# Slot lists of a mixture-of-experts router: ranks written 128 columns wide and in two parts, half the products, and the last transposes ahead of the last tile's first logits

## The chip, the cores and the metric

The kernel runs on one core of a Trainium2 chip. The metric is the device time of one execution in microseconds, as a median of several runs. The engines are TensorE (PE, with its weight loads shown apart as PEld), VectorE (DVE), ScalarE (ACT), GpSimd (POOL) and SyncE (SP), which here only issues transfers. TensorE's clock has two levels, 2.4 and 1.2 GHz; the profile shows what was granted as 1.00 and 0.50.

## The reference

Two layers of a bidirectional encoder over 512 tokens of width 1024, float32 throughout. Each layer mixes the tokens (four head groups and an output projection) and then runs a mixture of experts: a group of 8 experts is chosen of 4, and in it the two best experts of 8. What matters here is the routing:

```
pg = softmax(ht @ rg_w + rg_b);  pg_top, g_sel = top_k(pg, 1)
le = (ht @ re_w + re_b).reshape(T, 4, 8);  le_sel = le[chosen group]
top_v, top_i = top_k(le_sel, 2)
expert_idx = g_sel * 8 + top_i;  gate = pg_top * softmax(top_v)
# tokens are grouped by expert; for each expert:
y = (silu(xe @ w_gate[e]) * (xe @ w_up[e])) @ w_down[e]
x = x + g2 * (sum of the two experts' y, times their gates)
```

The kernel keeps 64 places (`CAP`) for the tokens of each of the 32 experts in its main pass. What overflows is handled behind it.

## The kernel before, in words

All engines run their own program; an order written out by hand and semaphores tie them together. Both layers have the same stages: modulation sums and projections, the Hyena filters, attention, the output projection `w_out`, the router, and then the stage of the 32 experts.

**End of the output projection (L842 to L866).** For each of four tiles of 128 tokens TensorE makes two halves of `w_out`; VectorE adds them to the residual `x_tok` (L2097, L2098) and raises `x_half` and then `x_ready`. TensorE turns the finished rows of a tile with `transpose_rows` (L640, four transposes for each half of the row), ScalarE copies them into `hT` (L1370), and eight products with `r_w` (`logits`, 36 columns) give a tile's logits. For the last tile TensorE's program was: `logits(b, 3, 0)`, then the transposes of the second half of the row, which wait for `x_ready`, then `logits(b, 3, 1)`, which waits until ScalarE has copied them. ScalarE computes the square sum of the same rows (L1523) ahead of that last copy. VectorE writes the normalised rows of the last tile (L1838) and then takes its logits (L2084).

**Choice and ranks (L2131 to L2162).** On VectorE a chain of some 20 small instructions finds the two experts of every token and writes them as one-hot rows `m1`, `m2`; their sum `msum` goes to TensorE (L870 to L874, bank `before`), which counts how many tokens with the same expert stand before each. From this VectorE makes each token's rank in its expert (`rank_tmp`, `rank_f`, L2158 and L2159), and compares the rank with 0 to 63 (L2160): `rank_is` holds for each of the 2 choices and 4 tiles a 128x64 matrix with a one at the token's rank. It lay in `pr_r` at 2304.

**The slot lists (L876 to L891).** A product of `rank_is` (stationary) with `id_of` (32 columns, one for each expert) puts the token's number at its place. It is made twice, once into rows 0 to 63 and once into rows 64 to 127 of the bank `slots`, as both halves of a row of 1024 values are gathered as rows of their own: `h_rows` are half rows. Eight pairs of such products add up. VectorE turns the result into `slot_i` (L2164), and POOL starts the gathers of the experts' tokens (L1689). Behind `slots`, VectorE makes the gates and `w_of` (L2167 to L2173), and TensorE makes the same products with `w_of` into `wslots`, followed by four products of `ones` with `msum` (the counts).

**The stage of the experts (L894 on).** It begins when VectorE has emptied `wslots` (L2179, L2180) and the first gather has landed: transposes (L900), a copy by ScalarE (L1534), 16 products with `w_gate` and 16 with `w_up` in 32 pieces of 256 columns, and so on. SP loads the weights, 3 MB for each expert, into four or six slots of `big`, `x_tok` and `mod`; a load waits until TensorE has used the slot's last content (L1152, L1158, L1164).

A float32 product shows as two MATMUL and two LDWEIGHTS instructions in the trace; a transpose as one of each.

Of the kernel before, what the change touches and what calls it, by code (L numbers as in the profile page):

```python
# [20 lines left out]
ALU = mybir.AluOpType  # L21
# [3 lines left out]
P = 128  # L25
DEPTH, D, S = 2, 1024, 512
NT = S // P
# [16 lines left out]
NE, NG, EPG, F = 32, 4, 8, 256  # L44
TURN = [EPG * (i % NG) + i // NG for i in range(NE)]
CAP = 64
# [39 lines left out]
def trunk(nc, a, out):  # L86
# [9 lines left out]
    with ctx:  # L96
# [15 lines left out]
        pr_r = sb("pr_r", [P, 3072])  # L112
# [12 lines left out]
        def at(buf, off, *dims, rows=P):  # L125
            n = int(np.prod(dims))
            v = buf[0:rows, off:off + n]
            if len(dims) == 1:
                return v
            names = "abcd"[:len(dims)]  # L130
            return v.rearrange(f"p ({' '.join(names)}) -> p {' '.join(names)}", **{names[i]: dims[i] for i in range(len(dims))})
# [63 lines left out]
        xg, yg = at(ht_r, 0, 4, S), at(ht_r, 2048, 4, S)  # L195
        xT = at(pr_r, 0, 2, KT * CAP)
        sil, act_h, act_T = at(pr_r, 1024, 2, F), at(pr_r, 1536, 2, F), at(pr_r, 2048, 2, P)
        rank_is = at(pr_r, 2304, 2, NT, CAP)
        rank_tmp = at(pr_r, 1792, 2, NT, NE)
        shift_w, shift_sum = at(pr_r, 2560, KT, 36), at(pr_r, 2560 + KT * 36, 36)  # L200
        next_parts = [part[0:4, :], at(pr_r, 2304, ADA, rows=4), at(mix_r, 0, ADA, rows=4)]
# [2 lines left out]
        def rb(*dims, rows=P):  # L204
# [8 lines left out]
        id_of, chosen, w_of = (row_tab[:, :, :, j] for j in range(3))  # L213
# [9 lines left out]
        rank_f = rb(2, NT)  # L223
# [35 lines left out]
        iota_c, iota_e = misc[:, 0:CAP], misc[:, 0:NE]  # L259
# [24 lines left out]
        dft_in, mod_in, ln2_in, mla_w_in, fill_in, rw_in, hot_ready, ov_i = (  # L284
            sem(n) for n in "dft_in mod_in ln2_in mla_w_in fill_in rw_in hot_ready ov_i".split())
# [231 lines left out]
        def _(pe):  # L517
            def mm(o, l, r, start=True, stop=True):
                return nc.tensor.matmul(o, l, r, start=start, stop=stop)  # L519
# [4 lines left out]
            def layer(l):  # L524
# [23 lines left out]
                if l == 0:  # L548
# [31 lines left out]
                    b = A.bank("fp")  # L580
# [9 lines left out]
                    b = V.bank("fn")  # L590
                    for j in range(4):
                        last = mm(b[:, j:j + 1], f_tmp[:, j * P:(j + 1) * P], ones[:, 0:1])
# [4 lines left out]
                    b = V.bank("fnb")  # L597
                    for j in range(4):
                        last = mm(b[:, j * P:(j + 1) * P], f_tmp[:, j * P:(j + 1) * P], ident[:, :])
# [25 lines left out]
                def transpose_rows(n, halves=range(2)):  # L625

                    t = n % NT
                    if n < NT:
                        pe.wait_ge(hrow_ready, 2 * NT * l + n + 1)
                    src = h_tok[:, t % 2, :] if n < NT else x_tok[:, t, :]  # L630
                    for half in halves:
                        if n >= NT:
                            pe.wait_ge(x_ready if half else x_half, NT * l + t + 1)
                        b = A.bank(f"hT{n}{half}")
                        for j in range(4):
                            if n < NT:
                                rows = src.rearrange("p (c k) -> p k c", k=KT)[:, 4 * half + j]
                            else:
                                rows = src.rearrange("p (h c j) -> p h j c", h=2, j=4)[:, half, j]
                            last = nc.tensor.transpose(b[:, j * P:(j + 1) * P], rows, ident[:, :])  # L640
                        last.then_inc(ready_a, 1)
# [15 lines left out]
                for m in range(6):  # L657
                    b = V.bank(f"d{m}")
# [173 lines left out]
                def logits(b, t, half):  # L832

                    taken(pe, f"hT{NT + t}{half}")
                    for k in range(4 * half, 4 * half + 4):
                        last = mm(b[:, 0:36], hT[:, k, t * P:(t + 1) * P], r_w[:, k, :], k == 0, k == KT - 1)
                    if half:
                        last.then_inc(ready_v, 1)
# [22 lines left out]
                            logits(b, t - 1, 1)  # L861

                b = V.bank(f"lg{NT - 1}")
                logits(b, NT - 1, 0)
                transpose_rows(2 * NT - 1, (1,))
                logits(b, NT - 1, 1)  # L866

                pe.wait_ge(m_ready, l + 1)
# [4 lines left out]
                    last = mm(b[:, n * NE:P], ones[:, :], ms[:, 0:P - n * NE], False, n == NT - 1)  # L873
                last.then_inc(ready_v, 1)  # L874

                pe.wait_ge(hot_ready, l + 1)  # L876
                b = V.bank("slots")
                for k in range(2):
                    for t in range(NT):
                        for rows in (slice(0, CAP), slice(CAP, P)):  # L880
                            last = mm(b[rows, 0:NE], rank_is[:, k, t], id_of[:, k, t], k + t == 0, k + t == NT)
                last.then_inc(ready_v, 1)
                pe.wait_ge(wtab_ready, l + 1)
                b = V.bank("wslots")
                for k in range(2):
                    for t in range(NT):
                        for rows in (slice(0, CAP), slice(CAP, P)):
                            mm(b[rows, 0:NE], rank_is[:, k, t], w_of[:, k, t], k + t == 0, k + t == NT)
                for t in range(NT):
                    last = mm(b[:, NE:2 * NE], ones[:, :], msum[:, t], t == 0, t == NT - 1)  # L890
                last.then_inc(ready_v, 1)  # L891
# [877 lines left out]
        def _(v):  # L1769
# [22 lines left out]
            def layer(l):  # L1792
# [356 lines left out]
                for o, mk in ((o1, m1), (o2, m2)):  # L2149
# [7 lines left out]
                cum_p = b[:, 0:P].rearrange("p (t e) -> p t e", t=NT)  # L2157
                step(TT(rank_tmp, chosen, twice(cum_p), ALU.mult))  # L2158
                step(RED(rank_f.rearrange("p k t -> p (k t)"), both(rank_tmp), X, ALU.add))  # L2159
                TT(both(rank_is), iota_c.unsqueeze(1).to_broadcast([P, 2 * NT, CAP]),  # L2160
                   rank_f.rearrange("p k t -> p (k t)").unsqueeze(2).to_broadcast([P, 2 * NT, CAP]), ALU.is_equal).then_inc(hot_ready, 1)
                took(STT(out=cum, in0=cum_p, scalar=float(NE), in1=iota_e.unsqueeze(1).to_broadcast([P, NT, NE]), op0=ALU.mult, op1=ALU.add))  # L2162
                b = V.take("slots")
                took(TS(slot_i[:, :], b[:, 0:NE], empty_half, None, ALU.add))  # L2164
# [162 lines left out]
```

## Time and profile before

| | |
|---|---|
| median of 3 runs | 1444.33 us (1442.68 to 1446.61) |
| the profiled execution | 1447.86 us, its span 1446.0 us |
| granted clock, mean | 0.964 |
| PE busy | 1295.3 us (90%) |
| PEld busy | 754.9 us (52%) |
| DVE busy | 642.6 us (44%) |
| ACT busy | 356.9 us (25%) |
| POOL busy | 274.5 us (19%) |
| DMA | 338.85 MB, mean 234 GB/s |

Times in the rows are microseconds from the start of the span. Busy time of PE says that something was in the array, not that it ran at its peak. 1.9 us lie outside the span.

### The profile page before, as it was taken

The numbers are of one execution on the slowest core, as the hardware profiler recorded it, in microseconds if no ns is written. First come the engines' busy times: TensorE is split into PE (matmuls) and PEld (weight loads), VectorE is DVE, ScalarE is ACT, GpSimd is POOL, SyncE is SP. The second block draws the span as 40 slices with busy tenths as digits, with TensorE's granted clock in tenths as the row PEclk, the third lists the DMA queues.
The fourth block names the chain that finished last, engine by engine and source line by source line (L and its number), as shares of the span: only waits on it lengthen the run. The fifth ranks groups of instructions, "written<-read, shape, count | busy, mean of one in ns | idle before, by whom it ended". The sixth has DMA issues, their size and how long they took to land.

```text
span 1446.0 us, 17998 instructions
## 1 busy us (share of the span) xinstructions
PE 1295.3 (90%) x6672; PEld 754.9 (52%) x6672; DVE 642.6 (44%) x1353; ACT 356.9 (25%) x839; POOL 274.5 (19%) x291
## 2 busy tenths in 40 slices
PE   5899999999997897898999999999999789997872
PEld 1445655766645554444444565566664555554441
DVE  4644547687535221433144263769853522221112
ACT  1411121556501111111221211145650111111111
POOL 0200310000100442332230022000010044332232
PEclk8999999999998899999999999999999789999997
DMA  8801222446675889999971132344137589999984
GB/s 289 323 36 58 87 106 103 181 161 208 223 294 204 326 311 370 409 407 404 380 280 46 59 145 76 118 174 146 59 117 288 204 314 388 399 401 402 400 328 145
DMA packets 100836, 338.85 MB, mean 234 GB/s; under 512 B 30084, under 2 KB 34820, under 8 KB 75498
## 3 DMA queue, kind: packets, MB, share of 16 engines
q1 hardware_dynamic: 75208, 307.55, 54.7%
q0 software_dynamic: 15072, 16.85, 5.2%
q10 hardware_dynamic: 10468, 13.28, 2.6%
q8 instruction: 55, 0.90, 0.2%
q14 instruction: 33, 0.27, 0.1%
HBM read 326.16 MB, written 29.00 MB: 246 GB/s over the span
## 4 chain that ended last, share of the span: by engine, by line
PE 80%; DVE 9%; ACT 4%; issue 4%; DMA 2%; POOL 1%; SPq 0%; ACTq 0%; POOLq 0%; DVEq 0%
PE bank L519 73%; PE bank L914 2%; PE bank L803 2%; DVE pr_r L2201 2%; ACT pr_r L1543 2%; DVE pr_r L2204 1%; PE bank L640 1%; DMA big<-in_ada_w_dram 1%; DVE small L2050 1%; DVE big L1783 1%; DMA x_tok<-x_rows 0%; POOL small L1623 0%; ACT ht_r L1469 0%; DVE ht_r L2045 0%; DVE part L1992 0%
## 5 line engine op out<-in xcount | busy, mean ns | idle before, releaser
L519 PE MATMUL bank<-big,pr_r 128*64 128x256 f32 (+2 forms) x3032 | 424.3, 399 | 44.7 <-DVE pr_r L2204 22.6
L519 PEld LDWEIGHTS bank<-big,pr_r 128*64 128x64 f32 (+1 forms) x3032 | 253.6, 152 | 184.9 <-issue 96.4
L519 PE MATMUL bank<-big,ht_r 128*128 128x512 f32 (+3 forms) x832 | 315.3, 555 | 3.0 <-ACT ht_r L1496 2.2
L519 PEld LDWEIGHTS bank<-big,ht_r 128*128 128x128 f32 (+1 forms) x832 | 147.0, 189 | 134.7 <-issue 119.4
L519 PE MATMUL bank<-big 128*128 128x256 f32 (+4 forms) x496 | 163.0, 466 | 8.7 <-ACT big L1343 3.6
L1698 POOL DMA_INDIRECT x_rows<-ht_r,slot_i x64 | 102.1, 1596 | 323.0 <-DVE ht_r L2207 309.5
L2201 DVE TENSOR_TENSOR pr_r<-pr_r,bank 64x256 f32<-64x256 f32 x65 | 27.5, 423 | 220.7 <-ACT pr_r L1543 215.7
L1543 ACT ACTIVATE pr_r<-bank 64x256 f32<-64x256 f32 x64 | 24.2, 378 | 405.4 <-PE bank L519 405.4
L519 PEld LDWEIGHTS bank<-big 128*128 128x128 f32 (+2 forms) x496 | 89.5, 192 | 48.3 <-issue 25.4
L2207 DVE SCALAR_TENSOR_TENSOR ht_r<-bank,mix_r,mod 128x512 f32<-128x512 f32 x65 | 48.8, 751 | 132.6 <-PE bank L519 132.6
L519 PE MATMUL bank<-ht_r,big 128*128 128x512 f32 x192 | 85.0, 605 | 1.4 <-ACT ht_r L1370 1.4
L1473 ACT ACTIVATE ht_r<-bank,small 128x512 f32<-128x512 f32 x96 | 65.4, 685 | 62.1 <-DVE small L2050 58.2
L1689 POOL DMA_INDIRECT ht_r<-h_rows,slot_i x64 | 68.1, 1064 | 47.8 <-DVE slot_i L2164 28.9
L2050 DVE TENSOR_REDUCE small<-bank 128x1 f32<-128x512 f32 x96 | 63.2, 686 | 18.1 <-PE bank L519 17.0
L803 PEld LDWEIGHTS bank<-ident,ht_r 128*128 128x128 f32 x336 | 39.0, 140 | 52.1 <-DVE ht_r L2061 19.7
L519 PEld LDWEIGHTS bank<-ht_r,big 128*128 128x128 f32 x192 | 37.1, 194 | 48.3 <-issue 46.3
L1661 POOL COPY ht_r<-small 128x1 f32<-128x1 f32 x32 | 5.5, 185 | 296.3 <-PE bank L803 296.3
L803 PE MATMUL bank<-ident,ht_r 128*128 128x128 f32 x336 | 54.9, 280 | 4.1 <-ACT ht_r L1473 1.3
L1992 DVE SCALAR_TENSOR_TENSOR part<-big,small,part 128x768 f32<-128x768 f32 x56 | 57.0, 1019 | 2.1 <-DVE mix_r L2075 0.2
L1534 ACT ACTIVATE pr_r<-bank 128x512 f32<-128x512 f32 x65 | 38.8, 597 | 49.0 <-PE bank L900 49.0
L1481 ACT ACTIVATE pr_r<-bank 128x512 f32<-128x512 f32 (+2 forms) x96 | 50.6, 534 | 0.0
L900 PE MATMUL bank<-ident,ht_r 128*128 128x128 f32 x260 | 49.1, 312 | 0.9 <-DVE mix_r L2180 0.9
(308 smaller groups left out, 1262.1 us busy)
## 6 DMA issues: line engine op xcount, KB each, us to landing
big<-in_moe_w_gate_dram SPq DMA_DIRECT2D x59, 1024.0 KB, 17.5
big<-in_moe_w_up_dram SPq DMA_DIRECT2D x59, 1024.0 KB, 21.4
big<-in_moe_w_down_dram SPq DMA_DIRECT2D x59, 1024.0 KB, 25.3
big<-in_ada_w_dram SPq DMA_DIRECT2D x16, 3072.0 KB, 12.0
big<-in_w_in_dram SPq DMA_DIRECT2D x4, 3072.0 KB, 14.1
big<-in_w_out_dram SPq DMA_DIRECT2D x4, 2048.0 KB, 8.6
mod<-in_ada_b_dram SPq DMA_DIRECT2D x12, 512.0 KB, 9.4
x_tok<-in_moe_w_gate_dram SPq DMA_DIRECT2D x6, 1024.0 KB, 16.0
```

The source lines that it names most:

```text
L519: return nc.tensor.matmul(o, l, r, start=start, stop=stop)
L803: last = nc.tensor.transpose(b[:, j * P:(j + 1) * P], prob[:, ms[0] % PB, j * P:(j + 1) * P], ident[:, :])
L900: last = nc.tensor.transpose(bank[b][:, j * P:(j + 1) * P], rows, ident[:, :])
L1473: A_(prob[:, n % PB, :], b[:, :], ACT.Exp, bias=nm[:, n:n + 1], accum_out=rs[:, n:n + 1]).then_inc(taken_a, 1)
L1481: A_(probT[:, n % TB, 0:w], b[:, 0:w], ACT.Copy).then_inc(taken_a, 1)
L1543: A_(sil[0:CAP, b, :], bank[2 + b][0:CAP, 0:F], ACT.Silu).then_inc(silu_ready, 1)
L1689: g.indirect_dma_start(out=xg[:, e % 4, :], out_offset=None, in_=half_rows(h2_rows), in_offset=bass.IndirectOffsetOnAxis(ap=slot_i[:, TURN ...
L1698: g.indirect_dma_start(out=half_rows(x_rows), out_offset=bass.IndirectOffsetOnAxis(ap=slot_i[:, TURN[e]:TURN[e] + 1], axis=0), in_=yg[:, e ...
L1992: return STT(out=part[:, :], in0=w, scalar=c_full[:, k:k + 1], in1=part[:, :], op0=ALU.mult, op1=ALU.add)
L2050: nc.vector.tensor_reduce(nm[:, n:n + 1], bank[4 + of(f"S{n}")[1] % 4][:, :], X, ALU.max, negate=True).then_inc(nm_ready, 1)
L2201: return TT(act_h[0:CAP, b, :], sil[0:CAP, b, :], bank[2 + b][CAP:P, 0:F], ALU.mult)
L2207: return STT(out=yg[:, b, :], in0=bank[6 + b % 2][:, :], scalar=w, in1=g2, op0=ALU.mult, op1=ALU.mult)
```

## The change

`rank_is` becomes 128 columns wide for each choice and tile, the ranks' comparison standing in it twice side by side, and moves to `pr_r` at 0. It is written by two instructions, one for each choice, of 128x512 elements each, and `hot_ready` is raised after each. One product now fills all 128 rows of the bank where two had filled 64 each: 8 in place of 16 in `slots`, and 8 in place of 16 in `wslots`. In the order of TensorE the transposes of the last tile's second half row come in front of `logits(b, 3, 0)`.

```diff
-        rank_is = at(pr_r, 2304, 2, NT, CAP)
+        rank_is = at(pr_r, 0, 2, NT, P)
...
                 b = V.bank(f"lg{NT - 1}")
+                transpose_rows(2 * NT - 1, (1,))
                 logits(b, NT - 1, 0)
-                transpose_rows(2 * NT - 1, (1,))
                 logits(b, NT - 1, 1)
...
-                pe.wait_ge(hot_ready, l + 1)
                 b = V.bank("slots")
                 for k in range(2):
+                    pe.wait_ge(hot_ready, 2 * l + k + 1)
                     for t in range(NT):
-                        for rows in (slice(0, CAP), slice(CAP, P)):
-                            last = mm(b[rows, 0:NE], rank_is[:, k, t], id_of[:, k, t], k + t == 0, k + t == NT)
+                        last = mm(b[:, 0:NE], rank_is[:, k, t], id_of[:, k, t], k + t == 0, k + t == NT)
                 last.then_inc(ready_v, 1)
                 pe.wait_ge(wtab_ready, l + 1)
                 b = V.bank("wslots")
                 for k in range(2):
                     for t in range(NT):
-                        for rows in (slice(0, CAP), slice(CAP, P)):
-                            mm(b[rows, 0:NE], rank_is[:, k, t], w_of[:, k, t], k + t == 0, k + t == NT)
+                        mm(b[:, 0:NE], rank_is[:, k, t], w_of[:, k, t], k + t == 0, k + t == NT)
...
-                TT(both(rank_is), iota_c.unsqueeze(1).to_broadcast([P, 2 * NT, CAP]),
-                   rank_f.rearrange("p k t -> p (k t)").unsqueeze(2).to_broadcast([P, 2 * NT, CAP]), ALU.is_equal).then_inc(hot_ready, 1)
+                for k in range(2):
+                    TT(rank_is[:, k].rearrange("p t (h c) -> p t h c", h=2), iota_c.unsqueeze(1).unsqueeze(2).to_broadcast([P, NT, 2, CAP]),
+                       rank_f[:, k].unsqueeze(2).unsqueeze(3).to_broadcast([P, NT, 2, CAP]), ALU.is_equal).then_inc(hot_ready, 1)
```

## Rows read from the trace of the kernel before

**Rows 1.** Page, part 4: the chain that ended last, by engine, by line.
```profile
PE 80%; DVE 9%; ACT 4%; issue 4%; DMA 2%; POOL 1%; SPq 0%; ACTq 0%; POOLq 0%; DVEq 0%
```

**Rows 2.** Timeline, layer 0's last logits; start, length, engine, line, what, idle before.
```profile
451.57 2.76 PE L519 MATMUL bank<-mix_r,ht_r 128*128 128x36 f32 x24
...
452.50 0.69 DVE L2098 TENSOR_TENSOR x_tok<-x_tok,pr_r 128x512 f32<-128x512 f32 x1
...
454.17 0.70 PE L640 MATMUL bank<-ident,x_tok 128*128 128x128 f32 x4
454.19 0.19 ACT L1523 ACTIVATION_READ_ACCUMULATOR big<-x_tok 128x1 f32 x1
...
454.91 0.60 ACT L1370 ACTIVATE ht_r<-bank 128x512 f32<-128x512 f32 x1 [0.54 <-PE bank L640]
455.38 1.41 DVE L1838 SCALAR_TENSOR_TENSOR big<-pr_r,small,mod 128x512 f32<-128x512 f32 x2 [0.65 <-POOL small L1623]
455.56 1.92 PE L519 MATMUL bank<-mix_r,ht_r 128*128 128x36 f32 x8 [0.69 <-ACT ht_r L1370]
...
457.52 0.26 DVE L2084 SCALAR_TENSOR_TENSOR mix_r<-bank,small,mix_r 128x36 f32<-128x36 f32 x1 [0.72 <-PE bank L519]
```

**Rows 3.** Timeline of PE, cut short: five of those eight products.
```profile
455.56 1.28 PE L519 MATMUL bank<-mix_r,ht_r 128*128 128x36 f32 x5 [0.69 <-ACT ht_r L1370]
```

**Rows 4.** Timeline, layer 0, from the ranks to the token list.
```profile
465.33 0.42 DVE L2159 TENSOR_REDUCE mix_r<-pr_r 128x8 f32<-128x256 f32 x1
465.79 0.69 DVE L2160 TENSOR_TENSOR pr_r<-misc,mix_r 128x512 f32<-128x512 f32 x1
466.40 0.28 DVE L2162 SCALAR_TENSOR_TENSOR mix_r<-bank,misc 128x128 f32<-128x128 f32 x1
466.53 1.92 PE L519 MATMUL bank<-pr_r 128*64 128x32 f32 x32 [1.69 <-DVE pr_r L2160]
468.57 0.25 DVE L2164 TENSOR_SCALAR slot_i<-bank,small 128x32 int32<-128x32 f32 x1 [1.90 <-PE bank L519]
```

**Rows 5.** Timeline, layer 0, from the first gather to the first expert.
```profile
469.76 1.32 POOL L1689 DMA_INDIRECT ht_r<-h_rows,slot_i  x1 [14.48 <-DVE slot_i L2164]
...
470.57 1.92 PE L519 MATMUL bank<-pr_r 128*64 128x32 f32 x32 [2.11 <-DVE pr_r L2173]
...
472.42 1.92 PE L519 MATMUL bank<-mix_r,ones 128*128 128x32 f32 x8
...
473.96 0.33 SPq L1158 DMA_DIRECT2D x_tok<-in_moe_w_up_dram  x1
...
474.81 1.10 PE L900 MATMUL bank<-ident,ht_r 128*128 128x128 f32 x4 [0.47 <-DVE mix_r L2180]
...
476.60 5.07 PE L519 MATMUL bank<-big,pr_r 128*64 128x256 f32 x32 [0.69 <-ACT pr_r L1534]
```

**Rows 6.** Windows: stretch, its length, busy time (count) of PE, PEld, DVE, ACT, POOL, granted clock, DMA share, GB/s.
```profile
466.50:468.50 2.00, 1.92 (x32) 1.79 (x32) 0.18 (x1) 0.00 (x0) 0.00 (x0) 0.50 1.02 430
...
472.40:474.40 2.00, 1.93 (x10) 1.78 (x8) 0.03 (x1) 0.00 (x0) 1.41 (x2) 0.50 0.36 107
...
1168.00:1169.00 1.00, 1.00 (x8) 0.57 (x6) 0.00 (x0) 0.00 (x0) 0.00 (x0) 0.52 0.36 148
1169.00:1170.00 1.00, 1.00 (x10) 0.56 (x7) 0.04 (x1) 0.30 (x1) 0.00 (x0) 1.00 0.00 0
...
1172.00:1173.00 1.00, 1.00 (x8) 0.41 (x6) 0.00 (x0) 0.00 (x0) 0.00 (x0) 1.00 1.08 459
```

**Rows 7.** Timeline, layer 1: last logits, first expert, first load of the next expert.
```profile
1142.08 1.92 PE L519 MATMUL bank<-mix_r,ht_r 128*128 128x36 f32 x8 [0.69 <-ACT ht_r L1370]
...
1163.11 6.54 PE L519 MATMUL bank<-big,pr_r 128*64 128x256 f32 x32 [0.69 <-ACT pr_r L1534]
...
1169.69 0.33 SPq L1152 DMA_DIRECT2D big<-in_moe_w_gate_dram  x1
```

**Rows 8.** SP's transfers in layer 0's expert stage, timeline.
```profile
535.59 0.33 SPq L1164 DMA_DIRECT2D big<-in_moe_w_down_dram  x1
...
545.71 0.36 SPq L1152 DMA_DIRECT2D big<-in_moe_w_gate_dram  x1
```

**Rows 9.** The chain that ended last, layer 0: a wait for weights.
```profile
564.18 4.83 issue
```

**Rows 10.** The same chain in layer 1: waits for weights, and 32 products at full clock.
```profile
1379.27 2.46 issue
1381.73 3.69 PE bank L519 x32
```

**Rows 11.** Windows of layer 1's expert stage, columns as in rows 6.
```profile
1170.00:1255.00 85.00, 77.25 (x547) 43.26 (x548) 17.70 (x37) 11.41 (x24) 38.41 (x31) 1.00 1.02 388
...
1305.00:1395.00 90.00, 70.02 (x472) 41.12 (x468) 15.31 (x33) 10.25 (x22) 28.16 (x22) 0.98 1.02 402
```

## The prediction

> **What bounds the kernel now.** I began with the page's chain of the work that ended last: TensorE carries 80% of it, VectorE 9% [rows 1]. That average says little about the router, so I read its stretch in the timeline, once for each layer. There the chain goes from engine to engine with nothing beside it: TensorE waits for VectorE's ranks, VectorE waits for the token list, TensorE waits for the gates, and the experts wait for both [rows 2, 4, 5]. Whatever is added between the last logits and the first expert is added to the time, unless the stage of the experts takes it back. The reader should look at the square brackets at the end of the rows: they name who was late. Then I read the granted clock of the stretch in the windows view: it is 0.50 (1.2 GHz) while both lists are made [rows 6].
>
> The sum is made against the profiled execution, 1447.86 us with a span of 1446.0 us, 3.5 us (0.24%) above the median of 1444.33 us. A difference of a few us is carried over to the median as it is.
>
> **The products for the lists.** A product is two instructions in the trace. Before, the token list takes 32 of them with 64 columns of weights each, in 1.92 us [rows 4]: 0.06 us each. After, it takes 16 with 128 columns of weights. What such an instruction costs here is shown three times. The counts behind the weight list have the very shape of the new products, 128 columns of weights and 32 moving ones: 8 in 1.92 us at clock 0.50 [rows 5, 6]. The last tile's logits, each with weights of its own: 8 in 1.92 us, and the first five of them in 1.28 us [rows 2, 3]. So one starts every (1.92 - 1.28) / 3 = 0.213 us, four times the cost of a narrow one, whose 32 start within 1.92 us. PEld is busy for 1.79 us with the 32 narrow loads and for 1.78 us with the 8 wide ones [rows 6]: the weight loads fill the time in both, and halving the count of the products does not halve it. The new list takes 1.92 + 8 x 0.213 = 3.62 us. Against 1.92 us that is **+1.70 us** a layer.
>
> The weight list is followed by the counts without a gap, 470.57 to 474.34 = 3.77 us in all [rows 5]. After it is 24 wide instructions in a row, 1.92 + 16 x 0.213 = 5.33 us: **+1.56 us** a layer. The difference from 1.70 is the step from narrow to wide, which disappears.
>
> The Trainium skill has rules on both sides. "TensorEngine Tiling (Array Packing)", section "Key Properties", says that tiles of the array work independently and can load weights and multiply in parallel, which speaks against merging the two halves; the trace agrees, with 32 narrow instructions in the time of 8 wide ones. Its section "Instruction Overhead" puts about 60 cycles on every matmul, which by itself would favour fewer of them; the wide rows, four times the narrow ones, do not follow it.
>
> **Ranks in two parts.** Each of the two new instructions writes 128x512 elements, as the old one did in 0.69 us [rows 4]. So the first is done when the old one was, and TensorE starts no earlier. The second ends some 0.6 us later and is needed when four products are through, 8 x 0.213 = 1.70 us after the start: hidden by them. Behind it on VectorE is only `cum` (L2162, 0.28 us), and then the wait for the token list, which now has 3.62 us of cover. Cost 0; if the broadcast over four dimensions made both instructions slower, the first of them would count, and I allow 0.0 to 0.3 us. If nothing covered it, the second would cost 0.6 us.
>
> **Transposes first.** Before, TensorE works on logits from 451.57, eight of whose 24 instructions belong to the last tile, and starts the transposes at 454.17; the rows are ready at 452.50 + 0.69 = 453.19 [rows 2]. The 16 instructions of the tile before end at about 453.3, so the transposes can start there and end at 454.0. But ScalarE is busy with the square sum until 454.19 + 0.19 = 454.38, and copies at 454.91 now: the copy comes at about 454.39, **0.52 us** earlier, not 0.87. The first logits of the last tile (8 x 0.11 us) fit in until 454.9, in front of the copy's end at 455.0. The second half is then 0.52 us earlier, and VectorE with it, as it is free from 455.38 + 1.41 = 456.79 and waits until 457.52 [rows 2]. At most 0.7 us can be gained, as VectorE's own rows come next. In this execution the clock fell just as these logits ran (they took 1.92 us in both layers [rows 2, 7]); where it falls later they take about half, VectorE is the last then, and the gain is 0. Range 0 to 0.7 us a layer; I take 0.5, by the copy of ScalarE.
>
> **Through to the experts.** The token list comes 1.70 - 0.5 = 1.2 us later, and so does the first gather [rows 5]. All of VectorE's work on the gates is queued behind `slot_i`, so the weight list starts 1.2 us later too, ends 1.2 + 1.56 = 2.76 us later, and its emptying releases the transposes (474.81 [rows 5]). The gather, which had landed by 473.96 (SP's load waits for it), is then not the last. The first expert starts **2.76 us** later in each layer.
>
> **Does the stage of the experts give it back?** In layer 0 it waits once for weights, 4.83 us [rows 9], for a load that SP issued at 545.71 behind small ones that began after the load at 535.59 [rows 8]. That one waits for TensorE's eighth expert, so this stall moves along with the delay. Layer 1 is bound by its transfers: share 1.02 from 1170 to 1395 [rows 11], with waits of TensorE near the end [rows 10]. But this stream begins when TensorE frees the first slot, at 1169.69 [rows 7], and the engines stand still just before it (share 0.36, then 0.00, then 1.08 [rows 6]). Freed 2.76 us later, it begins and ends later.
>
> **Sum**: 2 x (1.70 + 1.56 - 0.5) = 5.5 us. 1447.86 + 5.5 = 1453.4 for the profiled execution, 1444.33 + 5.5 = **1449.8 us** for the median, 0.38% slower. Its own range: gain of the transposes 0 to 0.7 (+1.0 / -0.4), ranks (+0.6), and where in the stretch the clock comes back. The first expert's 32 products took 5.07 us in layer 0, 6.54 us in layer 1 [rows 5, 7], and 3.69 us at full clock [rows 10]: a swing of 1.5 us a layer from one execution to the next, less in a median. 1447 to 1453.5.
>
> **Rivals.**
> (a) The clock comes back earlier (0.08). TensorE now has 5.33 us of wide products without a gap in front of the first expert. If that brought the clock up before it, each layer would save 5.07 - 3.69 = 1.4 and 6.54 - 3.69 = 2.9 us: 1449.8 - 4.3 = 1445.5, no change. Against it: 3.77 us without a gap left it at 0.50, and only the expert's own products brought it back.
> (b) Layer 1's transfers hide that layer's delay (0.06), for which their stream would have to start by something other than the first expert: 1444.33 + 2.76 = 1447.1, no change. Against it is the idle stretch at 1169.
> (c) Wide loads of ranks cost what two narrow ones do, 2 x 0.06 = 0.11 us (0.05): the lists would stay as they are, less the 0.14 us of the step: 1444.33 - 2 x 0.64 = 1443.0, no change. All wide rows at clock 0.50 speak against it. The Trainium skill, "TensorE: Matmul & The Clock Gate", section "LDWEIGHTS (loading the stationary operand)", puts a load at columns / 1.2 in ns, which would be an estimated 107 ns here and gives this case; the trace disagrees with 213 ns.
> (d) The other side: the number of instructions decides, and a wide one costs 0.06 us as a narrow one does (0.03). Then each list saves 16 x 0.06 = 0.96 us: 1444.33 - 2 x (1.92 + 0.5) = 1439.5, faster. It decides as soon as a wide instruction takes under 0.12 us, the price of the pair that it replaces; the rows say 0.213.
>
> **How the numbers follow.** Forecast 0.78, a 0.08, b 0.06, c 0.05, d 0.03. A measurement of this kernel can tell 0.3%, 4.3 us, from no change. The forecast's 5.5 us is only just beyond; with its spread some 0.78 of it counts as slower (0.61) and the rest as the same. Same: 0.17 + 0.08 + 0.06 + 0.02 = 0.33. Faster: d, half of c (the gain of the transposes added to a little luck) and a rest: 0.06. The range takes in a and b and the forecast's own: 1445.5 to 1453.5.
>
> **What would show it.** Right: 16 instructions in about 3.6 us between the ranks and `slot_i`; 24 in about 5.3 us in front of the emptying of `wslots`; from the last copy of `hT` to the first expert 2.8 us more than before, in both layers; clock 0.50 through it. Wrong: wide instructions spaced by 0.11 us or less, clock at 1.00 before the first expert, or the transposes not followed at once by the copy. If the first expert starts 2.8 us later and the end does not, (b) holds.

## The result and the profile after

The changed kernel takes 1450.36 us (median of 8 runs) against 1446.87 us of the kernel before (8 runs, the three of the table among them): ratio 1.0031, interval 1.0020 to 1.0042, or 4.5 us more (2.9 to 6.1) where 5.5 were forecast. The two medians alone lie 3.5 us apart, inside that interval. A second group of runs on another chip gave 1449.53 against 1446.65 us: 1.0024 (1.0010 to 1.0039). The profiled execution took 1450.29 us, its span 1448.5 us.

All times of the router are given below from **the anchor**: the start of the logits behind the last product of `w_out`, 451.57 in layer 0 [rows 2] and 1138.09 in layer 1 of before, 452.33 and 1139.25 after. The timeline of the changed kernel, layer 0 (start, length, engine, line, what, idle before and its releaser):

```profile
452.33 1.87 PE L519 MATMUL bank<-mix_r,ht_r 128*128 128x36 f32 x16
...
454.05 0.72 PE L640 MATMUL bank<-ident,x_tok 128*128 128x128 f32 x4
454.61 2.14 PE L519 MATMUL bank<-mix_r,ht_r 128*128 128x36 f32 x16
454.95 0.19 ACT L1521 ACTIVATION_READ_ACCUMULATOR big<-x_tok 128x1 f32 x1
455.04 0.58 ACT L1368 ACTIVATE ht_r<-bank 128x512 f32<-128x512 f32 x1
...
456.14 1.42 DVE L1836 SCALAR_TENSOR_TENSOR big<-pr_r,small,mod 128x512 f32<-128x512 f32 x2 [0.64 <-POOL small L1621]
457.47 0.25 DVE L2082 SCALAR_TENSOR_TENSOR mix_r<-bank,small,mix_r 128x36 f32<-128x36 f32 x1
...
465.72 1.29 DVE L2159 TENSOR_TENSOR pr_r<-misc,mix_r 128x512 f32<-128x512 f32 x2
466.56 3.59 PE L519 MATMUL bank<-pr_r 128*128 128x32 f32 x16 [1.78 <-DVE pr_r L2159]
...
470.26 0.25 DVE L2163 TENSOR_SCALAR slot_i<-bank,small 128x32 int32<-128x32 f32 x1 [3.04 <-PE bank L519]
...
472.25 3.62 PE L519 MATMUL bank<-pr_r 128*128 128x32 f32 x16 [2.10 <-DVE pr_r L2172]
...
475.69 1.89 PE L519 MATMUL bank<-mix_r,ones 128*128 128x32 f32 x8
...
478.06 1.10 PE L898 MATMUL bank<-ident,ht_r 128*128 128x128 f32 x4 [0.47 <-DVE mix_r L2179]
...
479.84 5.68 PE L519 MATMUL bank<-big,pr_r 128*64 128x256 f32 x32 [0.69 <-ACT pr_r L1532]
```

Read it beside [rows 2, 4, 5]. Each list has 16 instructions in place of 32 and takes 3.6 us in place of 1.92. The products of the first expert start 27.51 us after the anchor in layer 0 and 27.59 in layer 1, against 25.03 and 25.02: +2.48 and +2.57 us. I call this length **the stretch**. VectorE's last logits (L2082) no longer wait for anything. The weight loads fill the time of the wide list, too: PEld is busy for 3.48 of its 3.59 us, and the clock is at 0.50 (columns as in [rows 6]).

```profile
466.50:470.20 3.70, 3.59 (x16) 3.48 (x16) 0.72 (x2) 0.00 (x0) 0.00 (x0) 0.50 1.01 427
```

The first expert of layer 1, and the windows over the end of its products (columns as in [rows 6]):

```profile
1166.84 5.22 PE L519 MATMUL bank<-big,pr_r 128*64 128x256 f32 x32 [0.69 <-ACT pr_r L1532]
...
1172.11 0.33 SPq L1150 DMA_DIRECT2D big<-in_moe_w_gate_dram  x1
...
1173.07 0.45 PE L912 MATMUL bank<-ident,pr_r 64*128 64x64 f32 x2 [0.32 <-DVE pr_r L2200]
```
```profile
1166.80:1170.00 3.20, 3.16 (x16) 1.83 (x18) 1.57 (x6) 1.28 (x1) 0.00 (x0) 0.50 0.72 294
1170.00:1172.00 2.00, 2.00 (x21) 1.09 (x18) 0.00 (x0) 0.00 (x0) 0.00 (x0) 0.99 0.03 8
```

The first expert's products start 2.57 us later from the anchor than before, but take 5.22 us where they took 6.54 [rows 7], because they are at full clock for a larger part. The clock came back at 1168.95 before (the window of 1168 to 1169 has 0.52, the next 1.00 [rows 6]), 30.9 us from the anchor, and at 1170.0 after, 30.8 us from the anchor: the same moment in this layer, though the work had moved by 2.6 us. In layer 0 it was not the same, as told below. The load that begins the stream of weights [rows 7] is late by 32.86 - 31.60 = 1.26 us only.

### The profile page after: what moved, and what is told of

Read it like the earlier page. It is cut to its first block, busy times and chain, and to the rows that moved or that the text cites. A ratio compares the mean times of both kernels' runs of the same rounds, so it can differ in the third digit from the quotient of the medians.

```text
span 1448.5 us, 17870 instructions
## 1 busy us (share of the span) xinstructions
PE 1296.0 (89%) x6608; PEld 762.0 (53%) x6608; DVE 643.7 (44%) x1355; ACT 356.5 (25%) x839; POOL 274.2 (19%) x291
## 4 chain that ended last, share of the span: by engine, by line
PE 79%; DVE 9%; issue 4%; ACT 4%; DMA 1%; POOL 1%; SPq 0%; ACTq 0%; POOLq 0%; DVEq 0%
PE bank L519 73%; PE bank L803 2%; PE bank L912 2%; DVE pr_r L2200 2%; ACT pr_r L1541 2%; DVE pr_r L2203 1%; DMA big<-in_ada_w_dram 1%; PE bank L640 1%; DVE small L2048 1%; DVE big L1781 1%; POOL small L1621 0%; DMA x_tok<-x_rows 0%; ACT ht_r L1467 0%; DVE ht_r L2043 0%; DVE part L1990 0%
## 5 line engine op out<-in xcount | busy, mean ns | idle before, releaser
L519 PE MATMUL bank<-big,pr_r 128*64 128x256 f32 (+2 forms) x3032 | 419.8, 395 | 48.1 <-issue 22.8
L2200 DVE TENSOR_TENSOR pr_r<-pr_r,bank 64x256 f32<-64x256 f32 x65 | 27.5, 423 | 219.3 <-ACT pr_r L1541 214.3
L1687 POOL DMA_INDIRECT ht_r<-h_rows,slot_i x64 | 67.9, 1061 | 49.7 <-DVE slot_i L2163 30.8
```

The costliest lines, as they stand in the source:

```text
L1687: g.indirect_dma_start(out=xg[:, e % 4, :], out_offset=None, in_=half_rows(h2_rows), in_offset=bass.IndirectOffsetOnAxis(ap=slot_i[:, TURN ...
L2200: return TT(act_h[0:CAP, b, :], sil[0:CAP, b, :], bank[2 + b][CAP:P, 0:F], ALU.mult)
```

## The experiments

Each is judged by the stretch of its profiled execution and by its time. "First expert done" is the start of the two transposes that follow its 32 products (L914 in before's lines), from the anchor. Both lengths come from one profiled execution for each group of runs; the ratios come from several executions.

**Transposes first alone.** The kernel before with this edit:

```diff
                 b = V.bank(f"lg{NT - 1}")
+                transpose_rows(2 * NT - 1, (1,))
                 logits(b, NT - 1, 0)
-                transpose_rows(2 * NT - 1, (1,))
                 logits(b, NT - 1, 1)
```

> The kernel before with the order of the transposes alone changed. Stretch meant below: from the start of the logits behind the last product of w_out to the start of the first expert's 32 products, 25.03 us in layer 0 and 25.02 in layer 1 of the kernel before, 27.51 and 27.59 in the changed one. Theory (transposes first save what ScalarE's copy comes earlier, up to what VectorE's own rows allow): the stretch shortens by 0.5 to 0.8 us in each layer, to 24.2 to 24.5; the time by 1.0 to 1.6 us, 0.9989 to 0.9993 of before. Rival (it only helps where the clock falls early): no change in the stretch of this execution where the clock is still 1.00 in the last logits.

The stretch is 24.20 us in layer 0 and 24.60 in layer 1, 0.8 and 0.4 us shorter. The time is 0.9971 of before (0.9961 to 0.9982): 4.2 us less where 1.0 to 1.6 were expected, so the time went beyond what the stretch explains. In layer 1 something new is last: the gather of the experts' tokens. The timeline of TensorE shows the wait for it in brackets:

```profile
1157.53 1.10 PE L900 MATMUL bank<-ident,ht_r 128*128 128x128 f32 x4 [0.74 <-DMA ht_r<-h_rows,slot_i]
1159.32 4.99 PE L519 MATMUL bank<-big,pr_r 128*64 128x256 f32 x32 [0.69 <-ACT pr_r L1534]
```

The first expert's products take 4.99 us there in place of 6.54 [rows 7]. The windows of the same kernel show why (anchor 1134.72):

```profile
1160.00:1162.00 2.00, 2.00 (x14) 1.05 (x12) 0.67 (x4) 0.57 (x1) 0.00 (x0) 0.50 0.95 399
1162.00:1164.00 2.00, 2.00 (x22) 1.27 (x18) 0.00 (x0) 0.00 (x0) 0.00 (x0) 1.00 0.99 418
```

The clock is back 27.3 us from the anchor, 3.5 us sooner than in layer 1 of before, for a start that is 0.4 us sooner. Over both layers the first expert is done 2.4 us sooner, which covers more of the 4.2 us than the stretch does.

**The same once more, and the changed kernel beside it**, on one chip.

> The transposes first alone, once more: the run before gave 0.9971 with a stretch only 0.4 to 0.8 us shorter a layer, which explains 0.9989 to 0.9994. Theory (the remainder came from the wait for weights at the 13th expert of layer 0 and the clock's fall in it, which differ from run to run and chip to chip): 0.998 to 1.000 here. Rival (the order saves something that the stretch does not show): 0.997 again.

> The changed kernel itself, on the chip of the next three. Theory (both stages lose 2.5 us and pass it on): the stretch is 27.5 us, the time 1.002 to 1.005 of before. If the stage of the experts took the delay back on this chip, 1.000 to 1.001.

The transposes first gave 0.9987 (0.9972 to 1.0001), the changed kernel 1.0024 (1.0010 to 1.0039), both as expected. Their stretches are 24.20 and 24.39 us, and 27.51 twice. The gain of the transposes alone is thus 1.9 us here and 4.2 us in the run above, and its size stays open. Between the two kernels, which differ by the products and the ranks alone, lie 1449.53 - 1443.92 = 5.6 us, for 6.4 us of stretch.

**Wide products alone.** The changed kernel with the old order of the transposes, `logits(b, 3, 0)` ahead of them.

> The changed kernel with the old order of the transposes: wide products and ranks in two parts alone. Theory (a wide instruction costs four narrow ones in weight loads): lists of 3.6 us in place of 1.92, the stretch is 28.3 us (25.03 + 1.67 + 1.55 + 0.1) in each layer, and the time 1.0045 of before (6.6 us) if all of it reaches the end. Rival (the expert stage takes part of it back): the stretch is the same 28.3, and the time grows by 3 to 5 us, 1.002 to 1.0035.

The time is 1.0042 of before (1.0029 to 1.0055), 6.1 us more, close to the 6.6 of the theory; the rival's 3 to 5 us lie in the interval of 4.2 to 8.0 as well. The stretch is 28.33 us in layer 0, as expected, but 27.52 in layer 1. There the clock was still up in the last logits, which then take 1.08 us and not 1.92:

```profile
1140.24 0.70 PE L640 MATMUL bank<-ident,x_tok 128*128 128x128 f32 x4
1141.63 1.08 PE L519 MATMUL bank<-mix_r,ht_r 128*128 128x36 f32 x8 [0.69 <-ACT ht_r L1368]
```
```profile
1141.00:1144.00 3.00, 1.08 (x8) 0.97 (x8) 2.38 (x8) 0.79 (x2) 0.35 (x1) 1.00 1.02 335
```

VectorE takes them 5.14 us after the anchor, as it does with the transposes first. So the new order gains 0.8 us where the clock has fallen by then and nothing where it has not. The kernel in quarters below, which has the old order too, shows both: 5.14 us in layer 0, where the clock fell 6.7 us after the anchor, and 5.95 in layer 1, where it fell after 3.5 us.

**Why a wide instruction costs four narrow ones.** Two kernels with the products of before in another order and in other shapes. The edits show one of the two lists; the other has the same change. First the halves apart:

```diff
-                for k in range(2):
-                    for t in range(NT):
-                        for rows in (slice(0, CAP), slice(CAP, P)):
+                for rows in (slice(0, CAP), slice(CAP, P)):
+                    for k in range(2):
+                        for t in range(NT):
```

> The kernel before with the same 16 narrow products for each list in another order: all for rows 0 to 63 first, then all for rows 64 to 127. Theory (two neighbouring narrow products go side by side, each in its half of the array's columns, and that is why 0.055 us is enough for one instruction): apart they cannot, an instruction takes 0.107 us, a list 3.5 us, the stretch about 28.3 us. Rival (0.055 us is simply the price of an instruction, whatever it loads): the lists stay at 1.92 us, the stretch at 25.0.

Then the quarters:

```diff
-                        for rows in (slice(0, CAP), slice(CAP, P)):
-                            last = mm(b[rows, 0:NE], rank_is[:, k, t], id_of[:, k, t], k + t == 0, k + t == NT)
+                        for g in range(4):
+                            last = mm(b[32 * g:32 * g + 32, 0:NE], rank_is[:, k, t, 32 * (g % 2):32 * (g % 2) + 32], id_of[:, k, t], k + t == 0, k + t == NT)
```

> The kernel before with each narrow product cut in two: four products of 32 columns of weights for each choice and tile, one for each quarter of the rows, 64 instructions a list. Theory (the time goes by columns of weights, shared out over the groups that go side by side): an instruction takes 0.027 us and a list about 1.8 us, or 1.0 to 1.8 if four go side by side and each costs 0.053. Rival (a floor of 0.055 us for any instruction): 64 x 0.055 = 3.5 us a list.

The same 32 instructions with their halves apart, with windows over them (the first bracket counts the MATMUL instructions in each):

```profile
466.70 3.22 PE L519 MATMUL bank<-pr_r 128*64 128x32 f32 x32 [1.69 <-DVE pr_r L2160]
```
```profile
466.70:467.70 1.00, 1.00 (x10) 1.00 (x10) 0.15 (x1) 0.00 (x0) 0.00 (x0) 0.50 0.97 401
467.70:468.70 1.00, 1.00 (x16) 1.00 (x15) 0.00 (x0) 0.00 (x0) 0.00 (x0) 0.50 1.09 459
```

Twice as many, in quarters:

```profile
467.33 0.95 PEld L519 LDWEIGHTS bank<-pr_r 128*32 128x32 f32 x64 [1.83 <-DVE pr_r L2160]
467.34 1.08 PE L519 MATMUL bank<-pr_r 128*32 128x32 f32 x64 [1.69 <-DVE pr_r L2160]
```

The order alone takes a list from 1.92 to 3.22 us, and 64 instructions in quarters take 1.08: 0.017 us each. A price for each instruction can't give that. Ten narrow instructions that can't pair fill the first microsecond, 0.10 us each, as the theory said (0.107). In the second, where the first half's products end and the second half's begin, more fit in, and the list takes 3.2 us in place of the 3.5 expected; its stretch is 27.5 us in place of 28.3. The quarters came out at the low end of what was expected (1.0 to 1.8 us), the case in which four go side by side.

So neighbouring products for different columns of the array run side by side, two or four of them, and a wide one has nobody beside it. Products for other columns of the array also add into other rows of the bank, and no run keeps the two apart; but the price without a neighbour goes with the number of weight columns, 0.10 us for 64 and 0.213 for 128, as that of a weight load would.

**Where the rest of the stretch's price is: the clock.** The changed kernel with products that nobody reads in TensorE's waits (128 weight columns and 384 moving ones, two instructions each):

```diff
+                def keep_busy(n):
+                    for _ in range(n):
+                        mm(bank[4][:, 0:3 * P], ones[:, :], mask[:, :])
+
+                keep_busy(8)
                 pe.wait_ge(m_ready, l + 1)
...
+                keep_busy(2)
                 b = V.bank("slots")
...
+                keep_busy(3)
                 pe.wait_ge(wtab_ready, l + 1)
```

> The changed kernel with products of 384 columns that nobody reads put where TensorE waits: 8 behind the last logits, 2 ahead of the token list, 3 ahead of the weight list. Theory (the wide lists are as dear as they are because the clock is at 0.50): with the clock back at 1.00 each list takes 16 x 0.107 + 0.2 = 1.9 us in place of 3.6, the first expert's 32 products 3.7 in place of 5.1 to 6.5. Rival (an instruction's price is latency of another kind): the clock is 1.00 and the lists still take 3.6 us. If the added work does not bring the clock back, the products only delay: 8 x 0.64 = 5.1 us fits into the wait of 5.4, and the stretch grows by under 1 us.

Timeline (PE) and a window of layer 1:

```profile
1145.32 5.41 PE L519 MATMUL bank<-mask,ones 128*128 128x384 f32 x16
...
1154.47 1.94 PE L519 MATMUL bank<-pr_r 128*128 128x32 f32 x16 [0.41 <-DVE pr_r L2167]
```
```profile
1154.00:1158.00 4.00, 3.59 (x23) 2.84 (x22) 2.40 (x10) 0.00 (x0) 0.39 (x1) 1.00 0.92 373
```

A wide list takes 1.94 us at full clock and 3.59 at half. Eight of its instructions less take 1.08 us at full clock (the logits of the wide kernel above), so one costs (1.94 - 1.08) / 8 = 0.107 us, against (3.59 - 1.89) / 8 = 0.213 at half. This part came out as expected. The first expert's products did not: 3.7 us were expected, and they took 5.18 us in layer 0 and 5.92 in layer 1, because the clock fell to 0.50 again just before them (at 1161.4 in layer 1, 20.3 us after the anchor). The stretch is 24.42 us in layer 0, where the clock was down for the first of the added products, and 22.57 in layer 1. The time, 1448.0 us beside a median of 1451.4 for the kernel before on that chip, is that of one execution and proves nothing by itself.

**A delay of known size.** The changed kernel with 20 more wide products ahead of the weight list, in one layer at a time:

```diff
+                if l == 1:
+                    for _ in range(20):
+                        mm(bank[4][:, 0:NE], ones[:, :], id_of[:, 0, 0])
                 pe.wait_ge(wtab_ready, l + 1)
```

> The changed kernel, in layer 0 with 20 more wide products of 32 columns between the token list and the weight list, whose results nobody reads. Theory (the expert stage of layer 0 passes a delay of its start on to the end, its one wait for weights moving along; small products leave the clock at 0.50): 40 instructions of 0.213 us, less the 2.1 us in which TensorE waited anyway, so 6.4 us more in the stretch from the last tile's logits to the first expert (27.5 to 33.9 us), and the end 6.4 us later than in the changed kernel: 1.0075 of before. Rival (the stage takes a part back, as the shorter wait for weights in the two profiles hints): 3 to 5 us at the end. Second rival (a long row of wide products brings the clock back): the 40 instructions take less than 8.5 us and the clock rises before the first expert.

> The same 20 products in layer 1 alone. Theory (the stream of weights starts with the first expert, so a delay of it is passed on, though transfers bound the rest): 6.4 us more in the stretch and 6.4 at the end, 1.0075 of before. Rival (transfers bound the stage from the last to the first, so its end stays where it is): 6.4 us more in the stretch and under 2 us at the end, 1.004 or less.

In layer 1:

```profile
1160.28 8.72 PE L519 MATMUL bank<-pr_r,ones 128*128 128x32 f32 x40
1168.81 3.60 PE L519 MATMUL bank<-pr_r 128*128 128x32 f32 x16
1172.22 1.90 PE L519 MATMUL bank<-mix_r,ones 128*128 128x32 f32 x8
```
```profile
1160.30:1168.80 8.50, 8.50 (x41) 8.50 (x42) 2.63 (x11) 0.00 (x0) 4.17 (x4) 0.50 0.46 162
1168.80:1174.00 5.20, 5.20 (x25) 5.18 (x25) 0.00 (x0) 0.00 (x0) 0.00 (x0) 0.50 0.67 279
```

The stretch grows by 6.3 us in layer 0 and 6.2 in layer 1. The times are 1.0069 (1.0053 to 1.0086) and 1.0063 (1.0048 to 1.0077), 10.0 and 9.1 us over before, so 5.5 and 4.6 us beyond the changed kernel's 4.5, which comes from another group of runs. The intervals hold the expected 1.0075, but in layer 0 the times alone don't exclude the rival of 3 to 5 us. For that the profiles speak. From the anchor of layer 0 to that of layer 1 the one with the delay in layer 0 has 699.58 us, the other 690.46: 9.1 us more for 6.3 us at the first expert's end, so nothing was taken back there; where the rest comes from is open. From the anchor to the span's end of layer 1, the profile with the delay there has 314.66 us and the one with it in layer 0 has 308.53: the 6.1 us arrive whole, in the stage whose transfers are the bound. The second rival of layer 0 fell too: 13.8 us of wide products without a gap left the clock at 0.50.

**Smaller pieces, and TensorE kept busy.** First the lists and the counts in quarters, with the transposes first:

> The kernel before with the lists in quarters (four products of 32 columns of weights side by side, 1.08 us a list as the look before showed), the counts behind them in quarters too, and the transposes first. Theory: the stretch is 25.03 - 2 x 0.84 (lists) - 1.2 (counts: 32 narrow instructions in 0.6 us in place of 8 in 1.92) - 0.0 to 0.8 (transposes) = 21.4 to 22.2 us, and the time 2 x 3.0 to 3.7 = 6 to 7.3 us less than before, 0.995 to 0.996. Rival (the gain is given back in the expert stage): the stretch is as short, but the time only 0.998.

1.0007 (0.9996 to 1.0019) where 0.995 to 0.996 was expected: nothing gained. The lists take 1.08 us in layer 0, but then come the counts (timeline of TensorE):

```profile
472.94 0.35 PE L519 MATMUL bank<-mix_r,ones 128*32 128x32 f32 x5 [0.41 <-issue]
473.70 0.35 PE L519 MATMUL bank<-mix_r,ones 128*32 128x32 f32 x5 [0.41 <-issue]
474.46 0.34 PE L519 MATMUL bank<-mix_r,ones 128*32 128x32 f32 x5 [0.40 <-issue]
```

Four to six short instructions, 0.41 us of nothing, and so on. In layer 1 the gaps begin inside the weight list, behind its first 48 instructions. The stretch is 25.08 and 25.06 us. No semaphore stands behind the gaps. That instructions did not come fast enough is my reading; no run shows it by itself. Then only the lists in quarters, the counts wide:

> The lists in quarters and the transposes first, the counts as before in four wide products. In quarters the counts' instructions came in bursts of five with gaps of 0.41 us. Theory (too many short instructions in a row outrun the supply of instructions; the lists' 128 are within it): lists of 1.08 us, counts of 1.9 us without gaps, the stretch 22.6 to 23.4 us, the time 0.996 to 0.998. Rival (the supply holds back here too): gaps in the counts or in the weight list, the stretch over 24 us and no gain.

0.9967 (0.9956 to 0.9979), stretches of 22.54 and 22.62 us, and no gap. That is what was expected, the stretches even slightly shorter than the 22.6 to 23.4 us:

```profile
468.47 1.08 PE L519 MATMUL bank<-pr_r 128*32 128x32 f32 x64 [2.13 <-DVE pr_r L2173]
469.48 1.92 PE L519 MATMUL bank<-mix_r,ones 128*128 128x32 f32 x8
```

On the same chip the transposes first alone had a median of 1443.92 us and this kernel 1441.83: 2.1 us for the quarters themselves.

And the narrow products with the ranks in two parts, the transposes first and TensorE kept busy:

> The kernel before with the transposes first, the narrow ranks in two parts, and products that nobody reads in TensorE's waits (6, 2 and 3 of 384 columns), which in the wide kernel brought the clock back to 1.00 and the lists from 3.6 to 1.9 us. Theory: narrow lists at full clock take about 1.1 us, the counts 1.1, the stretch is 20.5 to 22.5 us against 25.0, and the time 0.993 to 0.997 of before. Rival (the first expert's products still run at 0.50 and the stage takes the rest back): the stretch is as short, and the time 0.998 or more.

0.9965 (0.9951 to 0.9980), as expected. A narrow list takes 1.12 us at full clock. The stretches are 22.90 and 22.13 us (20.5 to 22.5 expected), no less, because the gather is last now, and the clock has fallen again before the first expert's products:

```profile
470.81 1.08 PE L519 MATMUL bank<-mix_r,ones 128*128 128x32 f32 x8
474.51 1.10 PE L908 MATMUL bank<-ident,ht_r 128*128 128x128 f32 x4 [2.62 <-DMA ht_r<-h_rows,slot_i]
```

**All kernels with several timed executions.** Differences from before, both layers added, in us:

| kernel | stretch | first expert done | time, from the ratio |
|---|---|---|---|
| changed | +5.1 | +4.4 | +4.5 (2.9 to 6.1) |
| changed, again | +5.0 | +3.8 | +3.5 (1.4 to 5.6) |
| transposes first | -1.3 | -2.4 | -4.2 (-5.6 to -2.6) |
| the same, again | -1.5 | -2.5 | -1.9 (-4.1 to +0.1) |
| wide only | +5.8 | +4.3 | +6.1 (4.2 to 8.0) |
| delay in layer 0 | +11.3 | +10.5 | +10.0 (7.7 to 12.5) |
| delay in layer 1 | +11.2 | +10.4 | +9.1 (7.0 to 11.2) |
| lists and counts in quarters | +0.1 | +1.2 | +1.0 (-0.6 to +2.8) |
| quarter lists | -4.9 | -4.5 | -4.8 (-6.4 to -3.0) |
| kept busy, narrow | -5.0 | -5.9 | -5.1 (-7.1 to -2.9) |

The first expert is done, before, at 31.10 and 32.57 us from the anchor; changed: 34.20 and 33.82; transposes first: 30.71 and 30.59. Both columns follow the time over a span of 15 us, so what is lost or won in the router arrives at the end. The first expert's end is 0.8 us from the measured value on average, the stretch 1.0 us: the times alone don't decide between them. For the end speak the profiles, in which the clock is seen to come back between the two. The first two columns rest on one profiled execution of the kernel before.

**When the clock comes back.** I read the moment in every profile without the added products of 384 columns: twelve profiles, 24 layers. Windows of 0.2 us show where the clock goes from 0.50 to 1.00; all times are from the anchor.

| the first expert's products start | layers | clock back |
|---|---|---|
| 22.5 to 25.03 | 9 | 27.1 to 28.0 |
| 25.02 to 28.3 | 13 | 30.4 to 31.6 |
| 33.7 and 33.8 (the two delays) | 2 | 37.1 and 37.6 |

The return comes in three groups with nothing between them, and inside a group it does not move along with the start. The kernel before stands at the border: its two layers start at 25.03 and 25.02 us, and the clock is back at 27.9 in one and at 30.9 in the other. The changed kernel lies in the second group with all four layers, the transposes first in the first group with all four. Why the groups lie where they do, no run shows.

## Why the prediction was right or wrong

**The price of the products: right.** Forecast 3.62 us for a list, measured 3.59; forecast 5.33 us for the second list and the counts, measured 472.25 to 477.58 = 5.33. The reason given was that the weight loads fill the time, and that products in different tiles can overlap; the halves apart and the quarters show both. Rivals (c) and (d) fall with the 0.213 us of a wide instruction.

With (c) falls the estimate of 107 ns that it took from the Trainium skill, "TensorE: Matmul & The Clock Gate", section "LDWEIGHTS (loading the stationary operand)": the runs show 0.107 us at clock 1.00 (kept busy), but twice as much at the 0.50 of this stretch. What the Trainium skill says in "TensorEngine Tiling (Array Packing)", section "Key Properties", that tiles load and multiply in parallel, agrees: 32 instructions in 1.92 us with the halves alternating, in 3.22 us apart.

**Ranks in two parts: right.** The two instructions take 1.29 us together, where one had taken 0.69; TensorE starts 0.84 us after the first began, and 0.74 before, a cost of 0.1 in the range of 0 to 0.3.

**Transposes first: right in kind, small in size.** The sum had 0.5 us, with a bound of 0.7. VectorE takes its last logits earlier by 5.95 - 5.14 = 0.81 in layer 0 and 5.95 - 5.20 = 0.75 in layer 1, just beyond the bound. ScalarE's copy came 3.34 - 2.71 = 0.63 us sooner from the anchor, as it began 0.1 us before the read of the accumulator had ended. And part of the logits moved into the time before the clock fell. VectorE's own rows (L1836) then set the moment, as the bound said; the logits' instruction began 0.1 us before their end. A gain of zero where the clock stays up is shown by layer 1 of the wide kernel.

**The stretch** was forecast at +2.76 a layer and came to +2.48 and +2.57; 0.3 of the difference in layer 0 is the transposes. One of the signs was put wrongly: from the last copy of `hT` to the first expert it wanted 2.8 us more. But the 0.5 us of the transposes are gained ahead of that copy, so the sum gives 1.70 + 1.56 = 3.3 there; measured in layer 0 were 479.84 - 455.04 = 24.80 us against 476.60 - 454.91 = 21.69, 3.1 more.

**The expert stage passes the delay on: right, but the delay was counted at the wrong place.** The step said that the first expert starts 2.76 us later and took this for its end. Between the two lies the return of the clock, which did not move along by the same amount. In layer 1 it stayed at 30.8 to 30.9 us from the anchor, so the expert was done only 1.25 us later; in layer 0 it was done 3.10 us later, as the clock came back 27.9 us from the anchor before and 31.6 after (windows, before and then after):

```profile
479.00:480.00 1.00, 1.00 (x10) 0.55 (x10) 0.00 (x0) 0.00 (x0) 0.00 (x0) 0.77 1.00 414
```
```profile
483.00:484.00 1.00, 1.00 (x8) 0.59 (x6) 0.00 (x0) 0.00 (x0) 0.00 (x0) 0.53 0.08 33
```

That takes 0.7 us off the 5.05 us of both stretches (1.2 in the second profile), and leaves 4.4 and 3.8 where 4.5 and 3.5 were measured. Layer 1 shows most clearly that the end is what counts. From the anchor to the end of the span it has 307.91 us before and 309.25 and 308.90 in the two profiles of the changed kernel: 1.34 and 0.99 more. That goes with the first expert's end (1.25 and 1.03 us later) and not with its start (2.57 and 2.49). The way from the first expert's end to the end of the span took 275.3 to 275.4 us in all three profiles; over the profiles of all kernels it varies more, from 274.6 to 276.2.

I had this swing only in the range, as chance from one execution to the next. For the changed kernel it is not: its two profiles agree to 0.4 us at the first expert's end, and those of transposes first to 0.1 us. For the kernel before it may be, as it stands at the border of two groups and has one profile. A layer of it with an early return makes the change cost 2.8 to 3.1 us, one with a late return 1.0 to 1.3. Rival (a), the clock coming back before the expert, is excluded: in the changed kernel it came back 2.9 to 4.1 us behind the start of the expert's products, and 13.8 us of wide products did not bring it back either.

**The wait for weights in layer 0** moves with the delay, as said, though not exactly: 4.83 us before [rows 9], 3.01 and 3.65 us in the two profiles of the changed kernel, 2.74 and 3.21 in those of transposes first. After the longest one the clock had fallen and 32 products took 6.63 us; after 3.01 us they took 3.67, after 3.65 us 5.36. On those 32 products before lost 3 us more than the changed kernel's first profile, so the profiles of before and after come closer to each other than the delay says: the 32nd expert's transposes are at 738.34 - 451.57 = 286.77 us from the anchor before, 740.69 - 452.33 = 288.36 after (rows of PE, before and after):

```profile
738.34 0.45 PE L914 MATMUL bank<-ident,pr_r 64*128 64x64 f32 x2 [0.94 <-DVE pr_r L2201]
```
```profile
740.69 0.45 PE L912 MATMUL bank<-ident,pr_r 64*128 64x64 f32 x2 [0.93 <-DVE pr_r L2200]
```

That is 1.6 us of the 3.1 at the first expert, and at the anchor of layer 1 only 0.4 are left (686.92 against 686.52 us from the anchor of layer 0). Read by itself this would mean that the stage gives the delay back. The comparison with transposes first says otherwise: there the same way takes 683.32 and 682.94 us, and 686.92 and 686.60 in the changed kernel, 3.6 and 3.7 us more for 3.5 and 3.3 us at the first expert's end. So the loss belongs to the single profile of before, and its cause stays open. Rival (b) is excluded by the delay in layer 1.

**The time: partly luck.** 1449.8 us were forecast and 1450.36 measured. But the median of before went from 1444.33 us with three runs to 1446.87 with eight, 2.5 us up, and the difference came out about 1 us smaller than forecast; the two errors nearly cancel. What the forecast should be judged by is the difference, 5.5 against 4.5 us (2.9 to 6.1).

## What to carry to other kernels

Products that fill only a part of the array's columns are cheap when their neighbours fill the other parts: before merging them to halve their count, compare the busy time of the weight loads, not the number of instructions. Where the clock is down between two stages, follow a delay to the end of the first heavy work behind it and not to its start, since the clock's return need not move with it: here starts between 25.06 and 28.3 us had it at 30.4 to 31.6, and starts up to 24.6 at 28.0 or sooner. Here the useful direction was the opposite one, smaller pieces side by side with the transposes first (0.9967, or 4.8 us of 1447).

## What the runs showed of the hardware that was not expected

- Four float32 products of 32 weight columns side by side: 64 instructions in 1.08 us at clock 0.50, 0.017 us each, against 0.06 us for 64-column ones in pairs (32 in 1.92 us), 0.10 for those that can't pair (32 in 3.22 us) and 0.22 for 128-column ones (16 in 3.59 us).
- After 132 instructions of 32 weight columns in layer 0 and 112 in layer 1, gaps of 0.4 us after every four to six of them; with 8 wide instructions in place of the counts' 32 short ones, none.
- TensorE worked without a gap for 13.8 us, and its clock was at 0.50 throughout (delay in layer 1). In the kernel kept busy it was at 1.00 in the lists.
- The clock came back in groups: 27.1 to 28.0 us from the anchor in nine layers, 30.4 to 31.6 in thirteen, 37.1 and 37.6 in two. First experts that started 2.6 us apart had it at the same moment (30.8 and 30.9 us), and one that started 0.4 us sooner had it 3.5 us sooner.
